# First feed-forward of a recurrent decoder: its second and third block's 14 pairs of weight tiles all by seven block products, with the weight sums made by VectorE

## The reference

```python
def swiglu_half(x, g, w_up, w_down):
    h = rmsnorm(x, g)
    gate, up = jnp.split(h @ w_up, 2, axis=-1)
    return x + 0.5 * ((jax.nn.silu(gate) * up) @ w_down)

for l in range(DEPTH):          # DEPTH = 2
    x = swiglu_half(x, p['ffn1_norm'][l], p['ffn1_w_up'][l], p['ffn1_w_down'][l])
    y, st = mixer(rmsnorm(x, p['mix_norm'][l]), l, lb_all[l], p, tuple(s[l] for s in states))
    x = x + y
    x = swiglu_half(x, p['ffn2_norm'][l], p['ffn2_w_up'][l], p['ffn2_w_down'][l])
```

## Time and profile before

| | |
|---|---|
| time, median of 3 runs | 2846.6 us (2843.3 to 2848.44) |
| profiled execution, its own time | 2846.17 us |
| its span in the profile | 2844.4 us |
| TensorE busy | 2810.3 us (99%), 24828 matmuls |
| VectorE busy | 1689.4 us (59%) |
| GpSimd busy | 1596.5 us (56%) |
| ScalarE busy | 950.6 us (33%) |
| chain that ended last | PE 93%, DVE 3%, ACT 1%, POOL 1%, issue 1% |

### The profile page before, as it was taken

How to read it: one execution, slowest core, us unless ns; L and a number is a source line. 1 busy time by engine, 2 the same in 40 slices (tenths; PEclk the granted TensorE clock), 3 DMA queues, 4 the chain that set the end, 5 groups by cost and what they waited for, 6 DMA issues and landing times.

```text
span 2844.4 us, 63198 instructions
## 1 busy us (share of the span) xinstructions
PE 2810.3 (99%) x24828; PEld 2766.3 (97%) x24828; DVE 1689.4 (59%) x2419; ACT 950.6 (33%) x1616; POOL 1596.5 (56%) x1466
## 2 busy tenths in 40 slices
PE   8999999999999999999999999999999999999998
PEld 7999999999999999999999999999999999999998
DVE  8554677545553578383784637766454446783645
ACT  4221233123152425151452414330412523452433
POOL 6666676556654674525464352766565556734343
PEclk9999999999999999999999999999999999999999
DMA  5796835665654655353444433355665557453532
GB/s 191 199 247 191 237 101 182 170 154 155 185 167 111 189 163 162 117 175 110 126 144 140 156 120 109 121 169 169 160 181 153 161 151 186 148 170 118 158 123 78
DMA packets 196956, 444.27 MB, mean 156 GB/s; under 512 B 13464, under 2 KB 57664, under 8 KB 195904
## 3 DMA queue, kind: packets, MB, share of 16 engines
q1 hardware_dynamic: 107360, 281.09, 30.4%
q0 software_dynamic: 40128, 125.83, 18.7%
q10 hardware_dynamic: 49248, 34.28, 4.0%
HBM read 422.64 MB, written 144.35 MB: 199 GB/s over the span
## 4 chain that ended last, share of the span: by engine, by line
PE 93%; DVE 3%; ACT 1%; POOL 1%; issue 1%; ACTq 0%; DVEq 0%; PEld 0%; POOLq 0%
PE dense L723 60%; PE SA L783 15%; PE SB L783 11%; POOL Wl L588 1%; PE SA L998 1%; PE SA L915 1%; PE SA L859 1%; PE SA L1001 1%; PE SA L903 1%; PE SA L846 0%; PE SA L920 0%; POOL Wh L586 0%; PE SB L1005 0%; PE SA L848 0%; PE SA L855 0%
## 5 line engine op out<-in xcount | busy, mean ns | idle before, releaser
L588 POOL TENSOR_TENSOR Wl<-raw,Wh 128x512 fp32r<-128x512 f32 x620 | 854.0, 1377 | 51.8
L586 POOL TENSOR_SCALAR Wh<-raw 128x512 fp32r<-128x512 f32 x620 | 450.9, 727 | 672.8 <-PEq L728 445.8
L723 PE MATMUL dense<-Hh,Wh 128*128 128x272 f32 x2768 | 585.8, 293 | 15.2 <-POOLq L590 10.1
L723 PE MATMUL dense<-Hh,Wl 128*128 128x272 f32 x2768 | 573.9, 289 | 0.5 <-issue 0.5
L723 PE MATMUL dense<-Hl,Wh 128*128 128x272 f32 x2768 | 572.6, 288 | 0.0
L723 PEld LDWEIGHTS dense<-Hh,Wh 128*128 128x128 f32 x2768 | 435.0, 189 | 25.7 <-issue 16.2
L723 PEld LDWEIGHTS dense<-Hl,Wh 128*128 128x128 f32 x2768 | 436.7, 189 | 0.0
L723 PEld LDWEIGHTS dense<-Hh,Wl 128*128 128x128 f32 x2768 | 434.0, 189 | 0.8 <-issue 0.8
L651 POOL TENSOR_TENSOR Sl<-pair,Sh 128x512 fp32r<-128x512 f32 x120 | 173.7, 1465 | 421.8 <-ACT Sh L1088 421.0
L723 PE MATMUL dense<-Ah,Wh 128*128 128x272 f32 x1408 | 291.9, 289 | 0.8 <-DVE X L1814 0.7
L723 PE MATMUL dense<-Al,Wh 128*128 128x272 f32 x1408 | 290.7, 288 | 0.0
(11 more groups left out here) (473 smaller groups left out, 6317.4 us busy)
## 6 DMA issues: line engine op xcount, KB each, us to landing
raw<-wst SPq DMA_DIRECT2D x276, 512.0 KB, 3.7
w_sums<-wst POOLq DMA_DIRECT2D x36, 1536.0 KB, 13.3
w_sums<-wst POOLq DMA_DIRECT2D x18, 2048.0 KB, 16.8
pair<-wst SPq DMA_DIRECT2D x120, 256.0 KB, 3.5
pair<-w_sums SPq DMA_DIRECT2D x60, 512.0 KB, 3.7
wsum<-w_sums SPq DMA_DIRECT2D x60, 512.0 KB, 3.6
w_sums<-w_sums POOLq DMA_DIRECT2D x12, 1536.0 KB, 9.0
wsum<-wst SPq DMA_DIRECT2D x60, 256.0 KB, 2.5
```

The source lines that it names most:

```text
L586: pool.tensor_scalar(Wh[:, j, cs], raw[:, j, cs], 1.0, 0.0, ALU.mult, ALU.add).then_inc(glink, 1)
L588: pool.tensor_tensor(Wl[:, j, cs], raw[:, j, cs], f32(Wh[:, j, cs]), ALU.subtract).then_inc(glink, 1)
L723: mm = pe.matmul(out[:, a, 0:HALF], w[:, ring, w0:w0 + 128], x[:, k, a * HALF:(a + 1) * HALF], start=(k == 0 and n == 0), stop=(k == nk - ...
```

## The change

In f = 0, blocks 1 and 2 have no dense pairs any more: their 14 pairs go by `products` as in the later feed-forwards. Block 0 stays as it was. The pairs by products are numbered by their hidden tile less two, so block 1 holds pairs 6 to 13 and block 2 pairs 14 to 19. The blocks of an even pair are loaded into `pair`, those of an odd pair into `raw`, the dense pieces' buffer, which is free there between the down tiles. VectorE makes the four sums (`late_sums`) and the low parts of A11, A12 and S3 (`late_low`), GpSimd the low parts of S2, S1, S4 and A22 (`late_lows`). SyncE loads both tiles of a pair when the low parts of the pair two before are made. The down pieces of blocks 1 and 2 are loaded when the last pair's low parts are made; the load of a block's first pair is issued ahead of the down pieces of the block before.

```diff
+LATE_DVE, LATE_POOL = (A11, A12, S3), (S2, S1, S4, A22)
...
+        def late_block(odd, t, c):
+
+            return raw[:, t, c * 512:(c + 1) * 512] if odd else pair[:, 2 * t + c, :]
...
+            def load_late(i, source):
+
+                lates_read(max(i - 1, LATE0))
+                for t in range(2):
+                    if i % 2:
+                        sp.dma_start(raw[:, t, :], wst[source + t, :, :]).then_inc(raw_pair_in, 16)
+                    else:
+                        sp.dma_start(pair[:, 2 * t:2 * t + 2, :].rearrange("p a c -> p (a c)"),
+                                     wst[source + t, :, :]).then_inc(pair_in, 16)
...
+                    else:
+                        for i in range(FAST_AT[b] + 1, FAST_AT[b + 1]):
+                            if i == FAST_AT[b] + 1:
+                                sp.wait_ge(raw_free, p0 + DOWN_AT[1][b - 1] + KT + RAW)
+                                sp.sem_inc(pair_began, 1)
+                            load_late(i, off + 2 * (i - FAST_AT[b]))
+                    if b < 2:
+                        load_late(FAST_AT[b + 1], off + 2 * nf + KT)
+                    if b:
+                        lates_read(FAST_AT[b + 1])
                     with sp.Fori(0, KT // 2) as i:
                         load_two(p0 + DOWN_AT[1][b] + i * 2, off + 2 * nf + i * 2, nf * P)
...
+            def late_lows(i):
+
+                for q in LATE_POOL:
+                    pool.wait_ge(q_hi, (PAIR0[0] + i) * 7 + (q + 1))
+                    pool.tensor_tensor(Sl[:, q, :], late_slot(i % 2, q), f32(Sh[:, q, :]),
+                                       ALU.subtract).then_inc(q_lo_pool, 1)
+
...
-                    for i in range(1 if b == 0 else 0, nf // 2):
-                        one(p0 + UP_AT[b] + 2 * i)
-                        if b or i > 1:
+                    for i in range(FAST_AT[b] + 1, FAST_AT[b + 1] if b else 0):
+                        late_lows(i)
+                        sums(1, c)
+                        c += 1
...
                     for m in range(KT):
                         one(p0 + DOWN_AT[1][b] + m, nf * P)
+                        if b < 2 and m == 2:
+                            late_lows(FAST_AT[b + 1])
...
+            def late_sums(i, a, three=True, last=True):
+
+                n, odd = PAIR0[0] + a + i, a % 2
+                B = [late_block(odd, t, c) for t in range(2) for c in range(2)]
+                lows = ONE + POOL0[0] + (a - 1) * len(LATE_POOL) + i * len(LATE_POOL)
+                first = a == LATE0 and isinstance(i, int) and i == 0
+                if three:
+                    dve.wait_ge(*late_landed(i, a))
+                    dve.sem_inc(dve_began, 1)
+                    dve.wait_ge(q_lo_pool, lows + (len(LATE_POOL) if first else LATE_POOL.index(S1) + 1))
+                    TT(wsum[:, 0, :], B[2], B[3], ALU.add).then_inc(w_sum, 1)
+                    dve.wait_ge(w_sum, n * 4 + 1)
+                    TT(wsum[:, 1, :], wsum[:, 0, :], B[0], ALU.add).then_inc(w_sum, 1)
+                    TT(B[2], B[0], B[2], ALU.add).then_inc(w_sum, 1)
+                if last:
+                    dve.wait_ge(q_lo_pool, lows + (len(LATE_POOL) if first else LATE_POOL.index(S4) + 1))
+                    dve.sem_inc(dve_began, 1)
+                    dve.wait_ge(w_sum, n * 4 + 3)
+                    TT(wsum[:, 2, :], B[1], wsum[:, 1, :], ALU.add).then_inc(w_sum, 1)
...
+                    if ahead and alternate:
+                        late_sums(i, a + 1, last=False)
                     product(n, 2)
                     dve.wait_ge(prod_copy, n * 2 + 1)
                     TT(U[:, h1], SA[:, 1, h0], U[:, h0], ALU.subtract).then_inc(prod_read, 1)
                     if ahead:
-                        low(f, a + i + 1, A11)
+                        next_low(A11)
...
                     if ahead:
-                        low(f, a + i + 1, S3)
+                        next_low(S3)
+                    if ahead and alternate:
+                        late_sums(i, a + 1, three=False)
                     product(n, 6)
```

More of the change, by code:

```diff
@@ L460, in slot, with late_slot, late_landed @@
             return pair[:, q, :] if q < S3 else wsum[:, q - S3, :]
+        def late_block(odd, t, c):
+            return raw[:, t, c * 512:(c + 1) * 512] if odd else pair[:, 2 * t + c, :]
+        def late_slot(odd, q):
+            if q in (S1, S2, S4):
+                return wsum[:, (S1, S2, S4).index(q), :]
+            return late_block(odd, *{A11: (0, 0), A12: (0, 1), S3: (1, 0), A22: (1, 1)}[q])
+        def late_landed(i, a):
+            if a % 2:
+                return raw_pair_in, (a - LATE0 - 1) * 16 + 32 + i * 16
+            return pair_in, a * 16 + 32 + i * 16
         block = ctx.enter_context(nc.Block())
@@ L754, in ffn, with fast @@
                 alternate = f == 0
-                def fast(i):
+                def fast(i, mixed=False):
                     n = PAIR0[f] + i
@@ L803, in ffn @@
                         up(3, 0)
-                    if alternate:
-                        with pe.Fori(1 if b == 0 else 0, nf // 2) as i:
+                    if alternate and b == 0:
+                        with pe.Fori(1, nf // 2) as i:
                             for j in range(2):
-                                up(UP_AT[b] + j, i)
-                            fast(HALF_AT[b] + i)
+                                up(UP_AT + j, i)
+                            fast(MIXED_AT - PAIR0[0] + i, mixed=True)
                     else:
@@ L1093, in first_highs, with late_high @@
                     high(f, 0, q)
+            def late_high(i, a, q):
+                n = PAIR0[0] + a + i
+                if q in (A11, A12, A22):
+                    act.wait_ge(*late_landed(i, a))
+                else:
+                    act.wait_ge(w_sum, n * 4 + {S1: 1, S2: 2, S3: 3, S4: 4}[q])
+                act.wait_ge(prod_done, n * 7 + (q + 1))
+                act.activation(Sh[:, q, :], late_slot(a % 2, q), ACT.Copy).then_inc(q_hi, 1)
             def ffn(L, t0, norm_no, which):
@@ L1200, in ffn @@
                     if b == 0 and f == 0:
+                        for q in range(7):
+                            late_high(0, LATE0, q)
                         act.preload_act_table_set(LN_EXP)
@@ L1710, in products, with next_low @@
                     U, V, G, root = tmp[:, 3, :], tmp[:, j, :], tmp[:, 4 + j, :], tmp[:, 2, :]
+                    def next_low(q):
+                        if not alternate:
+                            low(f, a + i + 1, q)
+                        elif q in LATE_DVE:
+                            late_low(i, a + 1, q)
+                    if ahead and alternate:
+                        late_sums(i, a + 1, last=False)
                     product(n, 2)
@@ L1718, in products @@
                     if ahead:
-                        low(f, a + i + 1, A12)
+                        next_low(A12)
                     product(n, 5)
@@ L1741, in products @@
                     if ahead:
-                        low(f, a + i + 1, A22)
+                        next_low(A22)
                     hidden_lo(t, j, hidden_at(i, a, b))
@@ L1808, in ffn @@
                         layer_bounds(L)
+                    if alternate and b == 0:
+                        for q in LATE_DVE:
+                            late_low(0, LATE0, q)
                     if b < 2:
```

92 lines of the change are left out of this document (61 added, 31 removed).

## The result

The changed kernel takes 2901.8 us (median of 6 runs, 2900.98 to 2909.08), the kernel before 2846.3 in the same comparison (2843.3 to 2848.44): a ratio of 1.0201 (95% interval 1.019 to 1.0211), 2% slower. The spans are 2900.4 against 2844.4 us, **+56.0**. Forecast were +29. The direction and the mechanism of the pair loop were right, the size was not, and the time lies 10 us above the range of 2854 to 2892.

The account below looks back on a forecast made before the run. The prediction took TensorE to bound the kernel before, and VectorE's cycle, taking turns with GpSimd, to set the new pair period. 2846.2 + 26.5 for the pairs + 3 for smaller terms gave 2875.7, say 2875 us; range 2854 to 2892.

Parts of the forecast that it names:

- The pairs: Pairs of blocks 1 and 2: 184.0 us at a period of 13.9, against 157.5 before, so +26.5 us.
- The walk: VectorE's instructions for one pair, summed in order: 10.92 us undisturbed, plus 2.94 held up by GpSimd, period 13.9 us.
- engines take turns: Low parts on VectorE and GpSimd exclude each other, so a pair needs 12.0 us where TensorE gives it 10.5.
- A couple of 1.73 us: One low part each on VectorE and GpSimd, taking turns: some 1.73 us together, of which 0.48 are VectorE's.
- It stops once a pair, before S3, for 3.4 us: In the pair loop TensorE stops once, before product S3, until VectorE has read S2: 3.4 us.
- Term (4): In the pairs, ScalarE's 11 copies of under 0.7 us each are hidden, adding nothing.
- the rival with the falling clock: TensorE falls to half clock at its stops in the pairs; 2982 us if it stayed; above 2895: chance 0.06.
- Term (1): Block 0's end: down pieces queue behind pair 6's load and down tiles start later; +1 us, 0.5 to 5.
- Term (2): Block 1's last pair: split instructions fall on VectorE's last cycle, the last hidden tile comes late; +2 us, 0 to 5.
- Block 2 nothing: Block 2's last pair has no sums or low parts after it, so its end adds nothing.
- longer period, 15 to 16: In the pair loop GpSimd blocks VectorE at each of four low parts: 2889 to 2901 us, chance 0.12.
- 12.0 us by the prediction's estimate: Per pair, 6.8 us of VectorE's SBUF instructions and 5.1 of GpSimd's laid end to end: the period's lower bound.

Follow-up runs that it names:

- e4: The changed kernel without GpSimd's four low parts of each of pairs 6 to 19, only its semaphore counted up: 2874.55 us.
- Runs 1 to 3: Changed kernel with block 0's first two down pieces loaded before pair 6: 2901.51 us; with VectorE's first additions to X moved ahead: 2899.22; with both: 2891.71.
- Runs 7 to 9: Semaphore increments added at the start of TensorE's program: 140 in the changed kernel, 2903.83 us; 116 in the kernel before, 2867.27; 256 there, 2875.56.
- run 5: The changed kernel with all seven low parts of pairs 6 to 19 made by VectorE, none by GpSimd: 2890.6 us.

## Why the prediction was right, and where it failed

**The pairs: right, the hundredths by luck.** Forecast +26.5 us, measured +24.9; period 13.9 forecast, 13.81 in the mean. The walk gave low A11 1.58, low A12 1.41, a gate held by 0.35 and a value by 0.8; the trace, start to start, has 1.71 and 1.36, and 0.42 and 0.63 over the undisturbed 0.72. That engines take turns on such instructions is shown by taking GpSimd's four low parts away (11.58), or to VectorE (12.13), or two of them (12.77): each of these moves shortens the period, though the last two give VectorE more instructions, and the rows of 0.68 and 1.79 us stand where the GpSimd instruction is absent or present. The undisturbed cycle was 10.92 in the walk and 11.58 in e4, and GpSimd's part 2.94 in the walk and 13.81 - 11.58 = 2.23 in the runs: the base was 0.7 cheap, the turns 0.7 dear, and that the two cancel is luck. (A couple of 1.73 us less GpSimd's 1.28 also leaves VectorE 0.45, not the 0.48 of the walk, which changes nothing.)

**"It stops once a pair, before S3, for 3.4 us": wrong in form, right in sum.** There are two stops of up to 1.7 and 1.3 us, since ScalarE's copy of A11 stands behind the hidden tile's high part. Term (4) called ScalarE hidden by its busy time, and the walk left its order out. The period doesn't care. Whether one stop of 3.4 us would have kept the clock is open: with two short ones it is at 1.00 through all of it, so the rival with the falling clock has no case in the loop.

**Term (1), block 0's end: +1 forecast (0.5 to 5), +15.1 measured. This is the step that failed most.** Three parts of it. The load: 1.5 MB queued together were put at 8 us (6.2 to 12) and took 12.2 from the first issue at 101.80 until the piece landed, beside an adding transfer issued at 101.63; TensorE's stop for it was 5.96 us. VectorE's queue was not in the sum at all: the change puts pair 6's sums and low parts ahead of the first addition to X, in an order that already held the constants, and GpSimd's splits hold many of these up; TensorE's stop was 6.70 us. And around each stop lie some us at the slow clock. Runs 1 to 3 show that load and queue each cost about the same: 5.0 and 4.8 us alone, 11.8 together.

**Term (2), block 1's end: +2 forecast (0 to 5), +4.1 measured,** in its range, by the mechanism named: a wait of 2.1 us for the hidden tile's low part, and the clock at 0.83 in the ten us after it. "Block 2 nothing" was 0.9.

**Everything behind: taken as 0, measured +11.3.** No step of the sum spoke of it. Runs 7 to 9 put it on the place of TensorE's instructions.

Sum of the four: 24.9 + 15.1 + 5.0 + 11.3 = 56.3, less 0.3 elsewhere. With term (1) at what it measured, the forecast would have been near 2890, inside its range; the mixers' part no row of before could have told.

**The rivals.** The time came out beside "longer period, 15 to 16" (2889 to 2901) and above 2895, which had a chance of 0.06 by the falling clock. Neither is what happened: the period is 13.8, and the clock never falls in the loop. What carried the time there was in no rival: block 0's end and the mixers.

**What stays open.** Why a given place of the instructions costs more in the mixers, and whether the period is 256 or 128. No run took block 1's and 2's ends apart. That the slow clock costs what is left of block 0's 15.1 us after the waits of 5.96 and 6.70 is read from the windows, not tested by itself.

## What to carry to other kernels

Before work is moved from the busiest engine to its helpers, add up what the helpers can't do at the same time: here two engines' SBUF instructions, laid end to end, needed 12.0 us by the prediction's estimate where 10.5 were allowed, and if they take turns no order of them fits. Walk every engine's order not only in the loop but at the seams: the instructions that a change puts ahead of an old one (a sum ahead of an addition, a load ahead of a piece) cost 20 of the 56 us here, where the loop begins and ends. An engine that is freed of a wait may issue its transfers sooner and closer together, as GpSimd in run 5, and the load beside them pays. And a difference in a stage whose code is the same may be the program's length: shift the old kernel's program before explaining it.

## What the runs showed of the hardware that was not expected

- The mixers, same code, take 1370 or 1371 us with TensorE's program at its old place, 256 instructions later or 262 earlier, and 1382 to 1387 us at a shift of 116 or -402.
- 116, 140 and 256 semaphore increments on TensorE at the start stand 0.15 us apart, so that even 116 take longer than the 9.4 us that it had to wait there; they moved its later work by 7.5, 10.4 and 29.5 us.
- TensorE's clock stayed at 1.00 through two stops of 1.1 to 1.7 us in each 13.8. Around a stop of 5.96 us it was at 0.50 from 114 to 120 us, and in the ten us behind one of 2.1 it was at 0.83 in the mean.
- A run of tiny VectorE copies (32x32) is held up by GpSimd's splits like large instructions: four of them took 2.19 us beside a split, and 0.78 us before, with GpSimd idle.
